# Samples' cross-attention scores, two samples at a time, moved into the prompt's four query blocks

## What is computed

```python
def cross_attn(h, kv, wq, wo):
    q = (h @ wq).reshape(B, T, X_HEADS, X_HD) * (X_HD ** -0.5)
    s = jnp.einsum('bqhd,bmhd->bhqm', q, kv[:, :, 0].astype(q.dtype)).astype(jnp.float32)
    p = jax.nn.softmax(s, axis=-1).astype(q.dtype)
    o = jnp.einsum('bhqm,bmhd->bqhd', p, kv[:, :, 1].astype(q.dtype)).reshape(B, T, X_HEADS * X_HD)
    return o @ wo
...
xp = xp + cross_attn(rms_norm(xp, norm_xattn[l]), mkv, xattn_wq[l], xattn_wo[l])
xs = xs + cross_attn(rms_norm(xs, norm_xattn[l]), cache_mem_kv[l], xattn_wq[l], xattn_wo[l])
```

## Time and profile before

| | us |
|---|---|
| median of 3 runs | 3124.72 (3117.11 to 3127.07) |
| the profiled execution | 3124.77 |
| its span, first to last instruction | 3123.1 |
| PE busy | 2549.9 |
| DVE busy | 1857.6 |
| ACT busy | 956.4 |
| mean granted TensorE clock | 0.889 of full |

### The profile page before, as it was taken

One profiled execution on the slowest core, in us unless ns is written; L12 is line 12 of the kernel. 1 busy time (PEld: TensorE's weight loads), 2 busy tenths in 40 slices (PEclk: granted clock), 3 DMA queues, 4 the chain that ended last, 5 costly groups with the idle time before them and its releaser, 6 DMA issues. The chain is left out here.

```text
span 3123.1 us, 44524 instructions
## 1 busy us (share of the span) xinstructions
PE 2549.9 (82%) x17937; PEld 1895.3 (61%) x17937; DVE 1857.6 (59%) x2163; ACT 956.4 (31%) x1338; POOL 179.1 (6%) x268
## 2 busy tenths in 40 slices
PE   5967887776876989998888858869489999999992
PEld 4756665275663668887677746745345565665661
DVE  4366786395432255433676665221478999989983
ACT  2102122001120010001222221200267887888861
POOL 1131001310100000000000000000100000000001
PEclk8978889855887989999899988879689999999996
DMA  4554323542503422223222212124379999999973
GB/s 148 144 170 164 115 95 103 142 107 75 189 28 112 157 82 85 89 92 109 82 111 86 112 58 82 54 94 149 127 285 375 399 376 379 391 382 384 387 281 89
DMA packets 156880, 537.70 MB, mean 172 GB/s; under 512 B 15787, under 2 KB 51543, under 8 KB 149057
## 3 DMA queue, kind: packets, MB, share of 16 engines
q1 hardware_dynamic: 122018, 439.46, 37.7%
q0 software_dynamic: 18528, 85.75, 8.2%
q10 hardware_dynamic: 16128, 9.64, 1.1%
HBM read 501.55 MB, written 45.80 MB: 175 GB/s over the span
## 5 line engine op out<-in xcount | busy, mean ns | idle before, releaser
L721 PE MATMUL vector_unit<-arena,weight_parts 128*128 128x260 bf16 (+1 forms) x3936 | 451.7, 278 | 39.0 <-DVEq L2265 17.1
L721 PEld LDWEIGHTS vector_unit<-arena,weight_parts 128*128 128x128 f16 (+1 forms) x3936 | 388.8, 99 | 97.0 <-DVEq L2265 17.2
L721 PE MATMUL scalar_unit<-arena,weight_parts 128*128 128x260 bf16 (+2 forms) x2496 | 305.6, 284 | 67.3 <-DVE arena L1856 67.3
L721 PEld LDWEIGHTS scalar_unit<-arena,weight_parts 128*128 128x128 f16 (+2 forms) x2496 | 248.0, 101 | 121.9 <-issue 45.4
L1313 PE MATMUL vector_unit<-weight_parts,arena 128*128 128x512 bf16 (+3 forms) x1536 | 317.9, 364 | 3.7 <-PE scalar_unit L1275 3.0
L1313 PEld LDWEIGHTS vector_unit<-weight_parts,arena 128*128 128x128 f16 (+1 forms) x1536 | 148.2, 98 | 149.9 <-issue 6.8
L2694 DVE SCALAR_TENSOR_TENSOR weight_parts<-stream_ring,weight_parts 128x2048 f16<-128x2048 f32 (+2 forms) x108 | 204.8, 1941 | 21.6 <-ACT weight_parts L1715 21.3
L2694 DVE SCALAR_TENSOR_TENSOR weight_parts<-arena,weight_parts 128x2048 f16<-128x2048 f32 (+2 forms) x106 | 196.5, 1898 | 26.7 <-ACT weight_parts L1715 26.7
L1128 PE MATMUL scalar_unit<-arena,weight_parts 128*128 128x260 bf16 (+1 forms) x1536 | 179.9, 279 | 10.1 <-ACT arena L1622 7.6
L1805 DVE TENSOR_TENSOR weight_parts<-stream_ring,weight_parts 128x4096 bf16<-128x4096 f32 (+3 forms) x45 | 184.2, 4094 | 1.5
L1356 ACT ACTIVATE squares<-residual 128x520 f32<-128x520 f32 x56 | 35.6, 637 | 459.1 <-DVEq L1867 402.9
(11 more groups left out here) (480 smaller groups left out, 3584.5 us busy)
## 6 DMA issues: line engine op xcount, KB each, us to landing
stream_ring<-in_expert_w_gu SPq DMA_DIRECT2D x80, 1024.0 KB, 9.2
arena<-in_expert_w_gu SPq DMA_DIRECT2D x80, 1024.0 KB, 9.2
arena<-in_expert_w_dn SPq DMA_DIRECT2D x64, 704.0 KB, 7.9
stream_ring<-in_expert_w_dn SPq DMA_DIRECT2D x64, 704.0 KB, 7.6
stream_ring<-in_mem_kv SPq DMA_DIRECT2D x16, 2048.0 KB, 7.7
stream_ring<-in_ffn_w_gu SPq DMA_DIRECT2D x11, 2048.0 KB, 7.8
stream_ring<-in_xattn_wkv SPq DMA_DIRECT2D x8, 2048.0 KB, 8.0
stream_ring<-in_w_in_odd SPq DMA_DIRECT2D x8, 2048.0 KB, 8.4
```

Source lines behind the costliest of these rows:

```text
L721: ins = mm(u[0:cols, a * 512:a * 512 + w], weight if i else weight.bitcast(F16), x.bitcast(F16) if j else x, start=(k == 0 and i + j == 0) ...
```

## The change

On TensorE, one scalar unit is taken before the blocks and held (`keys`). In each block, after `scores(qb + 1)` and before the wait for the block's probabilities, `sample_scores(qb)` accumulates two samples' scores into it. The blocks' own transposes use the other scalar unit alone. After the fourth pair TensorE waits for its own matmuls before it frees the slot. On VectorE, the building of `QXP` moves ahead of the first block; after the blocks VectorE copies the held unit to `XS` and frees it. ScalarE skips the held unit in its turns, and in the last block waits for one more count, since the samples' scores count on the same semaphore.

```diff
+            def sample_scores(pair):
+                s, filled = next_slot("memkv")
+                pe.wait_ge(sem(f"slot_ready{s}"), filled)
+                mk = slot_view(s, 2, DC, MEM)
+                for b in (2 * pair, 2 * pair + 1):
+                    for c in range(DC):
+                        ins = mm(keys[0:32, 0:MEM], QXP[:, b * DC + c, :], mk[:, b % 2, c, :], start=(b == 0 and c == 0),
+                                 stop=(b == NB - 1 and c == DC - 1))
+                if pair < NB // 2 - 1:
+                    ins.then_inc(sem(f"slot_free{s}"), 1)
+                else:
+                    ins.then_inc(sem("scalar_unit_ready"), 1)
+                    pe.wait_ge(sem("scalar_unit_ready"), keys_full)
+                    pe.sem_inc(sem(f"slot_free{s}"), 1)
+
+            pe.wait_ge(sem("scalar_unit_free"), due("scalar_unit_free"))
+            keys = take_unit["scalar"]()
+            keys_full = due("scalar_unit_free", 0) + QB - 1
+            key_units.append((keys, keys_full))
             scores(0)
             for qb in range(QB):
                 if qb + 1 < QB:
                     scores(qb + 1)
+                if qb == 0:
+                    pe.wait_ge(sem("qxp_ready"), due("qxp_ready"))
+                sample_scores(qb)
                 pe.wait_ge(sem("xprobs"), due("xprobs"))
                 pe.wait_ge(sem("scalar_unit_free"), due("scalar_unit_free"))
-                u = take_unit["scalar"]()
+                take_unit["scalar"]()
+                u = other(keys)
...
-            pe.wait_ge(sem("qxp_ready"), due("qxp_ready"))
-            pe.wait_ge(sem("vector_unit_free"), due("vector_unit_free"))
-            u = take_unit["vector"]()
-            for b in range(NB):
-                if b % 2 == 0:
-                    s, filled = next_slot("memkv")
-                    pe.wait_ge(sem(f"slot_ready{s}"), filled)
...
-                for c in range(DC):
-                    ins = mm(u[0:32, 0:MEM], QXP[:, b * DC + c, :], mk[:, b % 2, c, :], start=(b == 0 and c == 0),
-                             stop=(b == NB - 1 and c == DC - 1))
```

On ScalarE:

```diff
+            keys = next_unit()
             exp_scores(0)
             for qb in range(QB):
...
-                act.wait_ge(sem("scalar_unit_ready"), due("scalar_unit_ready"))
-                u = next_unit()
+                act.wait_ge(sem("scalar_unit_ready"), due("scalar_unit_ready") + (qb == QB - 1))
+                next_unit()
+                u = other(keys)
```

On VectorE the memset of `QXP`, the wait for `qx_ready`, the 32 copies and the post of `qxp_ready` move unchanged from after the blocks to before `shift_scores(0)`; and after the blocks:

```diff
-            dve.wait_ge(sem("vector_unit_ready"), due("vector_unit_ready"))
-            u = next_unit()
-            V.tensor_copy(XS, u[0:32, 0:MEM]).then_inc(sem("vector_unit_free"), 1)
-            dve.wait_ge(sem("vector_unit_free"), sent("vector_unit_free"))
+            u, filled = key_units[l]
+            dve.wait_ge(sem("scalar_unit_ready"), filled)
+            V.tensor_copy(XS, u[0:32, 0:MEM]).then_inc(sem("vector_steps"), 1)
+            dve.wait_ge(sem("vector_steps"), sent("vector_steps"))
+            dve.sem_inc(sem("scalar_unit_free"), 1)
```

More of the change, by code:

```diff
@@ L465, in rows_after, with other @@
         return (b + 1, c - 3) if kind == "gu" and c in (3, 4) and b + 1 < BLOCKS else None
-    conv_units = []
+    conv_units, key_units = [], []
+    def other(unit):
+        return psum_s[1] if unit is psum_s[0] else psum_s[0]
     CHUNKS = [(c,) for c in range(4)] + [(4,), (5, 6), (7,), (8, 9)] + [(c,) for c in range(10, 16)] + [(), ()] + [(c,) for c in range(16, 32)]
@@ L1055, in cross @@
                 ins.then_inc(sem("vector_unit_ready"), 1)
-            pe.wait_ge(sem("qxp_ready"), due("qxp_ready"))
-            pe.wait_ge(sem("vector_unit_free"), due("vector_unit_free"))
-            u = take_unit["vector"]()
-            for b in range(NB):
-                if b % 2 == 0:
-                    s, filled = next_slot("memkv")
-                    pe.wait_ge(sem(f"slot_ready{s}"), filled)
-                    mk = slot_view(s, 2, DC, MEM)
-                for c in range(DC):
-                    ins = mm(u[0:32, 0:MEM], QXP[:, b * DC + c, :], mk[:, b % 2, c, :], start=(b == 0 and c == 0),
-                             stop=(b == NB - 1 and c == DC - 1))
[L1067 to L1072, removed]
             pe.wait_ge(sem("xs_probs"), due("xs_probs"))
@@ L1576, in cross @@
                 act.sem_inc(sem("xprobs_T"), 1)
+            due("scalar_unit_ready")
+            sent("scalar_unit_free")
             act.wait_ge(sem("xs_max"), due("xs_max"))
@@ L2280, in shift_scores @@
                 dve.wait_ge(sem("xmax"), sent("xmax"))
+            V.memset(QXP[:, :, :], 0.0).then_inc(sem("vector_steps"), 1)
+            dve.wait_ge(sem("vector_steps"), sent("vector_steps"))
+            dve.wait_ge(sem("qx_ready"), due("qx_ready"))
+            for b in range(NB):
+                for h in range(4):
+                    ins = V.tensor_copy(QXP[:, b * DC + 2 * h:b * DC + 2 * h + 2, 4 * b + h], QX[:, 2 * h:2 * h + 2, S + b])
+                    ins.then_inc(sem("vector_steps"), 1)
+                    dve.wait_ge(sem("vector_steps"), sent("vector_steps"))
+            dve.sem_inc(sem("qxp_ready"), 1)
             shift_scores(0)
@@ L2298, in cross @@
                 dve.wait_ge(sem("vector_unit_free"), sent("vector_unit_free"))
-            V.memset(QXP[:, :, :], 0.0).then_inc(sem("vector_steps"), 1)
+            u, filled = key_units[l]
+            dve.wait_ge(sem("scalar_unit_ready"), filled)
+            V.tensor_copy(XS, u[0:32, 0:MEM]).then_inc(sem("vector_steps"), 1)
             dve.wait_ge(sem("vector_steps"), sent("vector_steps"))
[L2301 to L2307, removed]
-            dve.wait_ge(sem("vector_unit_ready"), due("vector_unit_ready"))
-            u = next_unit()
-            V.tensor_copy(XS, u[0:32, 0:MEM]).then_inc(sem("vector_unit_free"), 1)
-            dve.wait_ge(sem("vector_unit_free"), sent("vector_unit_free"))
+            dve.sem_inc(sem("scalar_unit_free"), 1)
             V.tensor_reduce(small[0:32, 104:105], XS, AX, ALU.max, negate=True).then_inc(sem("vector_steps"), 1)
```

## The result

The changed kernel took 3031.40 us (median of 5 runs, 3029.56 to 3050.19), the kernel before 3121.37 (5 runs, 3117.11 to 3127.07): a ratio of 0.9723 with a 95% interval of 0.9691 to 0.9755. It is faster, by 86.5 us by the ratio, where 84.8 were forecast. The time of 3040 that was forecast is 9 us too long, inside the range of 3028 to 3067.

What follows compares the result with a forecast made beforehand. Bound: engines waiting in turn inside the cross-attention blocks, then the sample stage running alone. Terms: -41.3 + 11.6 - 13.0 + 0.3 = -42.4 us a layer, -84.8 for both, from 3124.8 to 3040.0; range 3028 to 3067.

Steps and rivals of the forecast that it cites:

- The sample stage that goes: Behind the fourth block: memset, small copies, sample scores and load waits leave this place, 41.3 us less a layer.
- The pairs and the clock in the blocks: In the four blocks: pairs beyond the holes add 11.6 us a layer; the clock staying at 1.00 gives back 13.0.
- TensorE's wait for its own last matmuls: In the fourth block, before the transposes: 0.3 us more a layer, range 0 to 1.2.
- The rival of the falling clock: In the blocks: clock falls in the new gap too, nothing given back, 3066.0 us; falling in some or all blocks, 0.31.
- `QXP`: Ahead of the first block: VectorE's memset and 32 copies are hidden with 0.1 us to spare, costed at nothing.
- the loads: Key and value loads for the samples: in their slots before they are needed, so no added wait.
- the held unit: The blocks' transposes have one scalar unit in place of two; it is always free, so no cost.
- The samples' value product: After the blocks: taken as unchanged, though it could cost 2.5 us less or 4.5 more.
- the rival of a clock that stays low: In the blocks: pairs and prompt scores at half clock, each block 13.4 us longer, 3150 us in all; chance 0.03.
- the gain given back by the experts' loads: Downstream, in the experts' stage: loads on their own schedule keep the end unmoved at 3124.8 us; chance 0.03.

Runs made afterwards that it cites:

- the half filled hole: The kernel before, with 8 f32 matmuls of unread result added in each block's 4.11 us hole ahead of the transposes: 3098.55 us, ratio 0.9915.
- the hole with a pair's work: The kernel before, with 16 f32 matmuls of unread result added in each block's hole, a pair's amount of work: 3116.70 us, ratio 0.9982.

## Why the prediction was right

- **The sample stage that goes.** The copy of the tile starts 0.02 us behind line 2320, and from the copy to the samples' value product are 2032.76 - 2027.64 = 5.1 us (4.9 before). Of the 41.3 us a layer nothing came back but 0.2.
- **The pairs and the clock in the blocks.** From the first scores to the end of the fourth value product were 67.8 and 68.1 us and are 66.8; the sum had 11.6 - 13.0 + 0.3 = -1.1. Value products at 3.84 (3.8 forecast), transposes at 1.09 (1.11), TensorE's wait for its own last matmuls 0.30 (0.3). The two large terms that nearly cancel were shown apart: the clock's by the half filled hole (12.8 and 13.0 us in the blocks), the pairs' by the step from there to the hole with a pair's work (11.4).
- **The rival of the falling clock.** The remaining gap, transposes and a wait, 2.3 us, leaves the clock at 1.00 in all eight blocks, here and in the kernels with filled holes. By the rule of the Trainium skill, "TensorE: Matmul & The Clock Gate", Part 4, the transposes would not have helped; the trace shows that the clock holds through this gap, and not whether transposes count. The prediction's step from that rule to its first rival was too quick: with the transposes taken as idle the gap is 2.3 us long, and an empty hole kept the clock at 1.00 for its first 2.2 us in the earlier trace rows and for all of its 4.11 us in the windows above, so the rule leaves it open whether the clock falls. That it holds in every block is measured and not explained. What brings it down is the empty 4.11 us with the transposes and the wait behind them: behind the value product, the pair leaves that hole open, and the clock falls in it or just after it.
- **`QXP`, the loads, the held unit.** The copies delay the first block by 0.1 us, where 0.1 to spare was forecast; nothing waits for it. No pair waits for a load; the only load left in layer 1's chain is the samples' third value load, which TensorE waits for by 0.7 us (0.8 before). The held unit costs no wait that the trace shows.
- **The samples' value product.** Taken as unchanged. Its first 32 records took 16.2 and 16.3 us before and take 15.3 to 16.9 in the profiles of the changed kernel; that is why one stretch is 1.5 us longer than the other.
- **The time.** Forecast was 3124.8 - 84.8. The stretches fell by 85.3, 85.2 and 84.4 in the three profiles. That these come within 0.5 us of 84.8 is partly luck, since in the first of them one layer gave 41.9 and the other 43.4 in place of 42.4 each. Of the 9 us between 3040 and the median of 3031, 3.4 are in the base, as the kernel before was timed at 3121.37 with two more runs, and 1.7 in the gain (86.5 by the ratio). The other 3.5 lie between the ratio and the two medians, well within the 17 us over which the untouched stages spread. That spread is wider than the 6 us that the forecast allowed for the runs.

Slower, the rival of a clock that stays low, and no change, the gain given back by the experts' loads, are both out: the pairs run at 7.0 us in every block, and the remainders stand around that of before.

## What to carry to other kernels

Work that has nothing to wait for is worth most in a hole of a dependent chain on the same engine, and there it can cost less than nothing, if the hole is what brings the clock down: look at the granted clock in the hole and behind it before pricing the move. Price such a move by the place, since the same matmuls a few lines later kept half the gain. And read a small change from its stretch in the trace, when the stages around it vary by more than the change is worth.

## What was not expected of the hardware

Matmuls whose result is thrown away made the kernel before faster: 16 records in each of eight holes, 8 x 3.5 = 28 us of TensorE work in all, for 27.7 us less in the two stretches. The clock did not fall at the same point of every empty hole of 4.11 us: in one it was at 0.50 after 2.7 us, and in another, with the pairs behind the value product, it stood at 1.00 through the whole hole and the transposes after it. And the same instructions in untouched stages take up to 17 us more or less from one execution to the next, with TensorE busiest in the two longest; the matrix-memory stage alone took 391.6 and 398.5.
